# S5's maps and first Toeplitz rows made pair by pair during the projection of gates, stored and loaded again

## The reference

```python
lam = lax.complex(a_re, a_im)
dt = jnp.exp(log_dt)[:, None]
a_bar = jnp.exp(lam * dt)
b_bar = ((a_bar - 1.0) / lam)[..., None] * b_mat
bu = jnp.einsum('bsgc,gnc->bsgn', u, b_bar)
_, states = lax.associative_scan(combine, (a_full, bu), axis=1)
y = jnp.einsum('bsgn,gcn->bsgc', states, c_mat).real
y = y + d_skip * u
```

## Time and profile before

| what | us |
|---|---|
| median of 3 runs (5352.08 to 5356.79) | 5355.65 |
| the profiled execution | 5355.36 |
| its span | 5353.3 |
| projection of gates (m = 10 to 13) | 915.2 to 1262.9 |
| S5: first DMA issued, last copy to yT done | 1269.85, 1478.68 |
| next stage's first instruction | 1485.89 |

### The profile page before, as it was taken

The page is one execution under the profiler, slowest core; times in us unless marked ns, Lnnn a source line. Parts: engine busy times, 40 slices in busy tenths (PEclk is TensorE's granted clock), DMA queues, the critical chain, the costliest instruction groups (busy, mean ns, idle before and its releaser), DMA issues.

```text
span 5353.3 us, 78359 instructions
## 1 busy us (share of the span) xinstructions
PE 4979.5 (93%) x29176; PEld 4435.0 (83%) x29176; DVE 3007.8 (56%) x5532; ACT 1724.3 (32%) x2713; POOL 924.7 (17%) x593
## 2 busy tenths in 40 slices
PE   8999999996689978696999999999999999999997
PEld 6888888885579957585998998989989999999997
DVE  4343331004656765254556666666677777777775
ACT  4121111111156821132223333333243433434443
POOL 0000000003111012133112213222122222122221
PEclk9999999998889989897999999999999999999998
DMA  3221212312144444444444545545466666666665
GB/s 131 75 79 66 94 68 77 103 69 71 48 163 139 149 153 140 157 134 149 150 157 149 184 166 167 176 158 183 167 216 221 206 214 219 221 232 222 221 210 183
DMA packets 252454, 814.55 MB, mean 152 GB/s; under 512 B 33660, under 2 KB 66167, under 8 KB 216056
## 3 DMA queue, kind: packets, MB, share of 16 engines
q1 hardware_dynamic: 213880, 685.39, 35.2%
q0 software_dynamic: 32656, 106.62, 8.5%
q10 hardware_dynamic: 5760, 20.45, 1.2%
HBM read 659.68 MB, written 154.71 MB: 152 GB/s over the span
## 4 chain that ended last, share of the span: by engine, by line
PE 46%; DVE 4%; ACT 1%; issue 1%; DMA 0%; POOL 0%; DVEq 0%; ACTq 0%; POOLq 0%
PE ex_g L2110 29%; PE ex_d L2124 16%; DVE ex_y L2259 2%; PE ex_g L2096 1%; ACT ex_wgh L2163 1%; DVE ex_wdl L2217 1%; DVE ex_wgl L2211 1%; DVE ex_t L2238 0%; DVE ex_bgu L2232 0%; DMA ex_nxt<-slots_d 0%; POOL ex_y L2066 0%; DMA ex_xg<-h_d,ex_nxt 0%; ACT ex_xh L2176 0%; POOL out L2069 0%; DVEq L2270 0%
## 5 line engine op out<-in xcount | busy, mean ns | idle before, releaser
L2110 PE MATMUL ex_g<-ex_xh,ex_wgh 128*128 128x256 f32 (+2 forms) x4352 | 1291.6, 297 | 72.4 <-DVE ex_t L2238 64.8
L2110 PE MATMUL ex_g<-ex_xl,ex_wgh 128*128 128x256 f32 (+2 forms) x4352 | 1283.8, 295 | 0.0
L2110 PE MATMUL ex_g<-ex_xh,ex_wgl 128*128 128x256 f32 (+2 forms) x4352 | 1283.6, 295 | 0.0
L2110 PEld LDWEIGHTS ex_g<-ex_xh,ex_wgh 128*128 128x128 f32 x4352 | 823.1, 189 | 102.1 <-issue 71.5
L2110 PEld LDWEIGHTS ex_g<-ex_xl,ex_wgh 128*128 128x128 f32 x4352 | 823.4, 189 | 8.5
L2110 PEld LDWEIGHTS ex_g<-ex_xh,ex_wgl 128*128 128x128 f32 x4352 | 824.5, 189 | 0.0
L2211 DVE TENSOR_TENSOR ex_wgl<-ex_wg,ex_wgh 128x2048 fp32r<-128x2048 f32 x274 | 626.5, 2287 | 55.0 <-ACT ex_wgh L2163 52.5
L2163 ACT ACTIVATE ex_wgh<-ex_wg 128x2048 fp32r<-128x2048 f32 x274 | 524.4, 1914 | 394.7 <-PE ex_g L2110 367.1
L2066 POOL TENSOR_SCALAR ex_y<-ex_y,ex_cur 128x1024 f32<-128x1024 f32 x82 | 295.1, 3599 | 1596.1 <-DVE ex_y L2259 1596.1
L2124 PE MATMUL ex_d<-ex_wdh,ex_ath 128*128 128x512 f32 x1312 | 523.4, 399 | 0.0
L2124 PE MATMUL ex_d<-ex_wdl,ex_ath 128*128 128x512 f32 x1312 | 515.6, 393 | 0.0
(11 more groups left out here) (371 smaller groups left out, 7931.0 us busy)
## 6 DMA issues: line engine op xcount, KB each, us to landing
ex_wg<-in_w_gu SPq DMA_DIRECT2D x276, 1024.0 KB, 4.9
ex_wd<-in_w_down SPq DMA_DIRECT2D x276, 512.0 KB
qkv_d<-prj_o SPq DMA_DIRECT2D x144, 256.0 KB, 2.0
att_blk<-qkv_d SPq DMA_DIRECT2D x48, 768.0 KB, 4.3
prj_raw<-in_w_in SPq DMA_DIRECT2D x112, 256.0 KB, 3.2
ex_bd<-in_b_down SPq DMA_DIRECT2D x34, 512.0 KB
gate_d<-prj_o SPq DMA_DIRECT2D x64, 256.0 KB, 2.0
mix_ring<-gate_d SPq DMA_DIRECT2D x32, 512.0 KB, 3.7
```

The lines of the kernel that those rows point to most:

```text
L2110: last = pe.matmul(gu[j][:, 0:size], w[:, k, j, :], x[:, k, 0:size], start=(k == 0 and x is xh and w is h), stop=(k == KD - 1 and w is l))
```

## The change

GpSimd gets a block in `project`. Once the bias rows are stored, it makes for each of the 16 pairs the output map (six instructions, 128x272) and the input map (six, 128x256), two pairs ahead at most. TensorE runs `pair(p)` behind the tiles t = 3, 6, 9 and 12 of m = 10 to 13: four transposes of the input map and two matmuls for the first rows. VectorE's `save_pair` copies both out of PSUM, adds the skip, and lays out the small blocks for pair p + 2. SP stores the three results to DRAM, the output map one tile and the rest two tiles after the pair. The buffers are parts of tiles that the projection uses only at its start. The c and d parameters are loaded at (1, 0).

In `s5` these computations go. SP loads inT, tab, the shifted first rows (now from DRAM) and cpad, by block; forward(b) on TensorE is turn_inputs, with chunk_states one pair behind; GpSimd zeroes intra first and then only orders tokens; VectorE only scans and copies yT, and its st memsets stand inside scan(0) and scan(1). The turned outputs have two PSUM banks. The sign of the imaginary part moves from cpad (with -1 there) to the state written by scan. The projection has 14 semaphores more than before (58), S5 has 9 fewer (28).

```diff
+        pair_at = {((CONST + p // 4), CONST_AT[p % 4]): p for p in range(PAIRS)}
...
+            @block.gpsimd
+            def _(pool):
+                go = Steps(pool, step_p)
+                def outer(dst, power, factor, p, n):
+                    return pool.tensor_tensor(dst[:, 0:n, :], power[:, p, 0:n].unsqueeze(2).to_broadcast([P, n, SC]),
+                                              factor[:, p, :].unsqueeze(1).to_broadcast([P, n, SC]), ALU.mult)
+                def output_map(p):
+                    z = p % 2
+                    if p >= 2:
+                        pool.wait_ge(cpad_out[z], 16 * (p // 2))
+                        pool.wait_ge(first_mm, p - 1)
+                    flat = lambda t: t.rearrange("p j c -> p (j c)")
+                    outer(ctmp[0], pr, cr, p, TS + 1)
+                    go(outer(ctmp[1], pi, ci, p, TS + 1))
+                    go(pool.tensor_tensor(cpad[z][:, 0, :], flat(ctmp[0]), flat(ctmp[1]), ALU.subtract))
+                    outer(ctmp[0], pi, cr, p, TS + 1)
+                    go(outer(ctmp[1], pr, ci, p, TS + 1))
+                    pool.tensor_tensor(cpad[z][:, 1, :], flat(ctmp[0]), flat(ctmp[1]), ALU.add).then_inc(cpad_ready, 1)
+                    pool.wait_ge(cpad_ready, p + 1)
+                def input_map(p):
+                    z = p % 2
+                    if p >= 2:
+                        pool.wait_ge(in_turned, p - 1)
+                    flat = lambda t: t.rearrange("p j c -> p (j c)")
+                    outer(itmp[0], rr, br, p, TS)
+                    go(outer(itmp[1], ri, bi, p, TS))
+                    go(pool.tensor_tensor(inm[z][:, 0, :], flat(itmp[0]), flat(itmp[1]), ALU.subtract))
+                    outer(itmp[0], rr, bi, p, TS)
+                    go(outer(itmp[1], ri, br, p, TS))
+                    pool.tensor_tensor(inm[z][:, 1, :], flat(itmp[0]), flat(itmp[1]), ALU.add).then_inc(inm_ready, 1)
+                    pool.wait_ge(inm_ready, p + 1)
+                pool.wait_ge(c_in, 48)
+                pool.wait_ge(rows_out, 16 * NG)
+                for p in range(PAIRS):
+                    output_map(p)
+                    input_map(p)
...
+                def store_map(p):
+                    sp.wait_ge(cpad_ready, p + 1)
+                    sp.dma_start(cpad_d[:, p, :, :], cpad[p % 2]).then_inc(cpad_out[p % 2], 16)
+                def store_pair(p):
+                    sp.wait_ge(inT_saved, p + 1)
+                    sp.dma_start(inT_d[:, p, :, :], inT).then_inc(inT_out, 16)
+                    sp.wait_ge(first_saved, p + 1)
+                    sp.dma_start(first_d[:, p, :], first_).then_inc(first_out, 16)
+                            for dst, src in ((cr, c_re), (ci, c_im)):
+                                sp.dma_start(dst[:, :, :], src).then_inc(c_in, 16)
+                            sp.dma_start(dsk[:, :], d_skip).then_inc(c_in, 16)
+                        if (m, t - 1) in pair_at:
+                            store_map(pair_at[m, t - 1])
+                        if (m, t - 2) in pair_at:
+                            store_pair(pair_at[m, t - 2])
...
+                def pair(p):
+                    z = p % 2
+                    pe.wait_ge(inm_ready, p + 1)
+                    if p:
+                        pe.wait_ge(inT_saved, p)
+                    for k in range(KT):
+                        for r in range(2):
+                            n = 2 * k + r
+                            last = pe.transpose(pt[0][:, n * P:(n + 1) * P], inm[z][:, r, k * P:(k + 1) * P], ident[:, :])
+                    last.then_inc(in_turned, 1)
+                    pe.wait_ge(blocks_ready, 4 * p + 4)
+                    pe.wait_ge(cpad_ready, p + 1)
+                    if p:
+                        pe.wait_ge(first_saved, p)
+                    for r in range(2):
+                        last = pe.matmul(pt[1][0:2 * SC, 0:W], bblk[z][:, r, :], cpad[z][:, r, 0:W], start=(r == 0),
+                                         stop=(r == 1))
+                    last.then_inc(first_mm, 1)
...
+                        if (m, t) in pair_at:
+                            pair(pair_at[m, t])
...
+                def blocks(p):
+                    for h in range(2):
+                        rows, cols = slice(SN * h, SN * (h + 1)), slice(SC * h, SC * (h + 1))
+                        dve.tensor_copy(bblk[p % 2][rows, 0, cols], br[rows, p, :]).then_inc(blocks_ready, 1)
+                        tsc(bblk[p % 2][rows, 1, cols], bi[rows, p, :], -1.0, None, ALU.mult).then_inc(blocks_ready, 1)
+                def save_pair(p):
+                    go_on = Steps(dve, step_f, 2 * p)
+                    dve.wait_ge(in_turned, p + 1)
+                    if p:
+                        dve.wait_ge(inT_out, 16 * p)
+                    dve.tensor_copy(inT, pt[0][:, :].rearrange("p (k n) -> p k n", n=P)).then_inc(inT_saved, 1)
+                    if p:
+                        dve.wait_ge(first_out, 16 * p)
+                    tt(skip, ident[0:2 * SC, 0:SC], ident[0:2 * SC, SC:2 * SC], ALU.add)
+                    dve.wait_ge(first_mm, p + 1)
+                    go_on(dve.tensor_copy(first_, pt[1][0:2 * SC, 0:W]))
+                    go_on(tt(skip, skip, dsk[:, p:p + 1].to_broadcast([2 * SC, SC]), ALU.mult))
+                    tt(first_[:, 0:SC], first_[:, 0:SC], skip, ALU.add).then_inc(first_saved, 1)
+                    dve.wait_ge(first_saved, p + 1)
+                    if p + 2 < PAIRS:
+                        blocks(p + 2)
...
+                        if (m, t - 1) in pair_at:
+                            save_pair(pair_at[m, t - 1])
...
                         if (m, t) == (BIAS, 6):
                             bias_rows()
+                            dve.memset(bblk[0], 0.0)
+                            go(dve.memset(bblk[1], 0.0))
+                            blocks(0)
+                            blocks(1)
...
-                def load_table(b):
+                def load_maps(b):
+                    q = slice(b * BP, (b + 1) * BP)
+                    if b >= 2:
+                        sp.wait_ge(x_mm, BP * (b - 1))
+                    sp.dma_start(inT[b % 2][:, :, :, :, :].rearrange("p q k r n -> p q (k r) n"), inT_d[:, q, :, :]).then_inc(
+                        map_in[b % 2], 16)
                     if b >= 2:
                         sp.wait_ge(st_ready, b - 1)
-                    sp.dma_start(tab[b % 2][:, :, :, :], tab_d[:, :, b * BP:(b + 1) * BP, :]).then_inc(tab_in[b % 2], 16)
-                def shift(b):
-                    sp.wait_ge(d_added, b + 1)
+                    sp.dma_start(tab[b % 2][:, :, :, :], tab_d[:, :, q, :]).then_inc(tab_in[b % 2], 16)
+                def load_outputs(b):
+                    q = slice(b * BP, (b + 1) * BP)
+                    sp.wait_ge(zeroed, 2)
                     if b >= 2:
                         sp.wait_ge(y_mm, BP * (b - 1))
                     for h in range(2):
                         for j in range(JT):
                             sp.dma_start(intra[b % 2][SC * j:SC * (j + 1), :, h, SC * j:W],
-                                         first[SC * h:SC * (h + 1), :, 0:W - SC * j]).then_inc(f_out[b % 2], 16)
+                    sp.dma_start(cpad[b % 2][:, :, :, :], cpad_d[:, q, :, :]).then_inc(cpad_in[b % 2], 16)
+                def store(b):
                     sp.wait_ge(o_saved, 4 * (b + 1))
                     sp.dma_start(y_out[:, b, :], yT[b % 2][:, :]).then_inc(y_stored[b % 2], 16)
+                load_tok(0)
+                load_maps(0)
+                load_tok(1)
+                load_maps(1)
+                load_outputs(0)
+                load_tok(2)
+                load_outputs(1)
+                load_tok(3)
+                for b in range(2, NB):
+                    load_maps(b)
+                    load_outputs(b)
+                    store(b - 2)
+                for b in range(NB - 2, NB):
+                    store(b)
...
-                order(0)
-                input_map(0)
                 for z in range(2):
-                    last = pool.memset(intra[z][:, :, :, :], 0.0)
-                last.then_inc(zeroed, 1)
-                for b in range(1, NB):
+                    pool.memset(intra[z][:, :, :, :], 0.0).then_inc(zeroed, 1)
+                for b in range(NB):
                     order(b)
-                    input_map(b)
...
-                    pe.wait_ge(inT_ready, p + 1)
-                    if q == 0 and b:
-                        pe.wait_ge(x_saved, 2 * b)
+                    if q == 0:
+                        pe.wait_ge(map_in[b % 2], 16 * (b // 2) + 16)
+                        if b:
+                            pe.wait_ge(x_saved, 2 * b)
...
                     for q in range(BP):
                         p = b * BP + q
                         turn_inputs(p)
-                        turn_map(p)
-                        first_rows(p)
-                        chunk_states(p)
+                        if q:
```

(83 more changed lines are left out.)

138 lines of the change are left out of this document (28 added, 110 removed).

## The result

The changed kernel takes 5288.16 us (median of 4, 5285.89 to 5292.11), the kernel before 5353.86 in the same series (5351.35 to 5356.79). The ratio is 0.9879, 95% interval 0.9866 to 0.9891: 1.2% faster. Forecast were 5299 and a range of 5285 to 5332, so the result lies near the low end of the range. The profiled execution took 5285.89 us, its span 5283.9.

What follows compares the result with a forecast made beforehand. TensorE, busy 93% of the span, was taken to bound the projection, and the chain of maps and scans S5. From 5355.4 us, -84 (S5) + 27.4 (pairs) + 0.5 (semaphores) = -56 gave 5299, range 5285 to 5332.

Steps and rivals of the forecast that it cites:

- The bound: Projection: TensorE is always busy and pays in full for added work; S5: the chain of maps and scans sets its time.
- The insertion: Projection: 16 pairs of transposes and matmuls on TensorE at 1.71 us each, 27.4 us in all, bounds 24.2 and 33.6.
- the upper bound of 33: GpSimd in the projection: 33 us a pair if quarter-size instructions kept all of their 2.74 us.
- The +0.5: Stage ends: 14 semaphores more to clear after the projection, 9 fewer after S5, 0.09 us each: +0.5 us.
- S5 by hand: S5's new chain laid out step by step from its first load: 125 us instead of 208.8, saving 84.
- the latencies: End of S5's laid-out chain: 3 us added for latencies left out, from 122 to 125.
- the upper bound of the saving: S5: at most 92 us saved, if there is no stall for the map of block 3.
- Late loads: Rival in S5: each of four blocks waits some 6 us for a map or cpad; saving 60, kernel 5323; chance 0.20.
- GpSimd's pace: Rival in the projection: GpSimd needs 23 us a pair against 16.3, kernel 5319; chance 0.07.
- Half clock: Rival in S5: TensorE runs at 1.2 GHz throughout, adding some 60 us, kernel 5359, no change; chance 0.04.
- Bound by transfers: Rival in S5: its 22.5 MB move at 94 GB/s and take 239 us, kernel 5413; chance 0.03.
- VectorE freed of GpSimd: S5: scans no longer run beside GpSimd; four rotations took 5.91 us beside it, 2.49 alone.

Runs made afterwards that it cites:

- e2: Projection of the changed kernel with the S5 of the kernel before, so maps are made in both places: 5383.60 us, ratio 1.0051.
- e6: Changed kernel with 24 more GpSimd multiplications a pair ahead of the two maps: 5337.51 us, ratio 0.9969.
- e8: e4 run again in the next series: 5286.46 us, ratio 0.9870.
- e4: Changed kernel with all stores behind all loads in SyncE's queue: 5282.87 us, ratio 0.9863.
- e5: Changed kernel with 27 GpSimd multiplies of 128x1024 in S5 that nobody reads: 5342.45 us, ratio 0.9978.
- e9: e5 with the same elements cut four times finer, 36 and 72 multiplies of 128x256: 5329.73 us, ratio 0.9952.
- e3: Changed kernel with one PSUM bank instead of two for the turned outputs: 5309.14 us, ratio 0.9913.

## Why the prediction was right

**The bound.** Both halves held: TensorE pays for the pairs one for one (e2: 28.7), and S5 gained more from TensorE's idle time (54.7 us) than from its work (37.0).

**The insertion.** 1.71 us a pair was forecast, 1.62 found. The joint ahead, 0.09, isn't there, the one behind is 0.11 as in the earlier trace rows. The matmuls that meet waits brought no further joints. 25.9 instead of 27.4, with 0.7 of idle time beside it.

**GpSimd.** 8 to 11 us a pair was the bound from the earlier trace rows; 8.56 was found, and the upper bound of 33 fell. e6 shows what the rival would have cost. VectorE's save_pair took 2.0 us, not 3 to 5, and GpSimd beside it slowed the splits only from 0.69 to 0.72 us.

**The end of the stage.** From S5's last copy to the next stage are 6.6 us (1414.54 to 1421.13), with nine semaphores fewer to clear, and 7.2 before. At the projection's end 14 more cost nothing: 6.95 us from the last matmul to S5's first load before, 6.89 now. The +0.5 came out as -0.6, and the 0.09 us a semaphore isn't borne out.

**S5 by hand**, in us from its first load, forecast and found:

| step | forecast | found | from |
|---|---|---|---|
| st_ready(0) | 30 | 29.4 | 1325.44 + 0.68 |
| outputs(0) done | 43.5 | 40.6 | 1337.24 |
| outputs(1) done | 63 | 63.8 | 1360.50 |
| turn_outputs(0) done | 66.5 | 66.9 | 1363.57 |
| chunk states of block 3 | 76.5 | 75.7 | 1372.41 |
| outputs(3) done | 112 | 109.8 | 1406.52 |
| last copy | 122 | 117.9 | 1407.23 + 7.31 |
| with latencies | 125 | 117.9 | |

The mechanism was right and the term of S5, -84, was mis-sized: it measured -91. Of the 7.1 us between, 3 are the latencies, which the rows I had used already held, and 1.9 are the tail, 8.0 us from outputs(3) to the last copy instead of 10: with two banks the copies run at 0.91, not at 1.1 us a group. The other 2.2 stood at the end of outputs(3), after errors that in part cancelled. outputs(0) was done 2.9 early: I had 31 for its loads, but they came before scan(0) was done, and TensorE waited for st_ready alone. That was lost again by outputs(1): forward(2) took 11.0 us instead of 7, with a wait of 2.3 for the map of block 2, which I had seen as just in time, and slow matmuls behind it. The map of block 3 was there 7.6 us after the last copy of block 0 instead of 9, and TensorE waited 6.9 for it.

So 5355.4 - 91 + 26.9 - 0.6 = 5291, with the 5288 measured; the rest lies in stages that the change doesn't touch. 5288 is also the very edge of the range that I had given the forecast (5288 to 5313). And the upper bound of the saving, 92 without a stall for the map of block 3, was too low: with that stall S5 saved 91, without it 98 to 100 (e8, e4), and e4's 5283 lies under the whole range.

**The rivals.** Late loads: two of the forwards waited, 9.2 us in all, not 24. GpSimd's pace: no wait. Half clock: 0.88 over S5, only the first matmuls behind each wait slow (0.52 from 1304 to 1311, 1.00 from there to 1321). Bound by transfers: the DMA queues moved 181 GB/s on average, and behind the first tokens TensorE waited for transfers only the 9.2 us above. What I had taken for a side note, VectorE freed of GpSimd, is a condition of the gain: e5 shows that 27 reading instructions of GpSimd beside the scans would have taken some 50 of the 65 us. From the earlier trace rows I had taken a factor of 2.4; it was 3.6 in e5, and 3.9 in the first scan of the kernel before.

## What to carry to other kernels

Work that waits at the head of a stage with idle engines is worth moving under a stage that one engine fills, if that engine's own share, here 1.6 us a pair, is small against the waits it ends; price the two halves apart, since they add. When a wait is removed, look next at what stands behind the wait in the same DMA queue: a store that waits for the last copies shouldn't stand ahead of the next block's load. And the helper engine's instructions beside a scan cost by their length, at each instruction of the scan.

## What the runs showed of the hardware

- VectorE and GpSimd instructions that both read SBUF held each other up by an amount that grows with the other's length: VectorE's with two inputs went from 0.69 us to 2.72 beside 128x1024 multiplies, about a whole one of them more, and to 1.10 beside 128x256 ones. A copy 128x1016 with one input went from 0.69 to 2.61 and 0.98; a memset stayed at 1.76 (e5, e9). The 128x256 multiplies took 0.99 at the mean, 0.62 in the projection.
- With pauses of 1.1 to 1.2 us between groups of four transposes TensorE fell to 1.2 GHz after two groups in the tails of e3 and of the kernel before (0.66 to 1.12 us; clock 0.50 from 1418 to 1429 in e3). Four groups with the same pauses stayed at 0.66 elsewhere in e3 (clock 1.00 from 1360 to 1366), and so did the tail with two banks, whose pauses are 0.2 to 0.7 us.
- In a dense stretch, a wait of 6.7 us was followed by some 6 us at 1.2 GHz (e6, clock 0.50).
- Foreign f32 matmuls between projection tiles cost 0.11 us a joint, behind them only; the bias rows had cost 0.09 ahead as well.
